# The moving operands of a two-layer decoder trunk 32 bytes past a multiple of 2 KB

## The chip, the cores and the metric

The kernel runs on one core of a Trainium2 chip. The metric is the device time of one execution in microseconds (us). Times come from runs of the kernel on the chip; the profile and the trace come from one more execution, recorded by the hardware profiler. The five engines are TensorE (PE, and PEld for its weight loads), VectorE (DVE), ScalarE (ACT), GpSimd (POOL) and SyncE (SP), which here only issues DMAs.

## The reference

The input x is one sequence of 256 tokens of width 2048, in float32. Two layers follow one another:

```
h = x
layer 0: h += gmlp_chunk_mixer(rms_norm(h))       # 2048 -> 4096 (u, v), gelu, layer norm of v,
                                                  # 16 causal 128x128 token mixes, u * v', 2048 -> 2048
         h += conv_ffn(rms_norm(h))               # gate and up 2048 -> 5632, causal conv of 3 taps
                                                  # on the gate, silu(gate) * up, down 5632 -> 2048
layer 1: h += dilated_attention_mixer(rms_norm(h))# qkv 2048 -> 9216, partial rotary, 3 dilations x
                                                  # 8 heads, merged by softmax, 1024 -> 2048
         h += conv_ffn(rms_norm(h))
out = rms_norm(h)
```

Everything is float32 in and out. The products with the stacked weights are nearly all of the work: each weight is read once, and multiplies 256 tokens.

## The kernel before

**Layout.** Activations are kept transposed: a block is 128 features (partitions) by 256 tokens, so a width of 2048 is KT = 16 blocks and the FFN's 5632 are FB = 44. Weights are tiles of 128 x 128, streamed in units of UT = 8 tiles (512 KB, 784 units in all) through a ring of RING = 4 slots.

**Split products.** Every float32 weight tile and every activation block is split in a high and a low part (float32r). ScalarE writes the high part of a weight unit (`w_hi`, L440), VectorE the rest (`w_lo`, L730). A block of activations has 512 columns: 256 of the high part, then 256 of the low part. For each weight tile TensorE runs a pair (in `multiply`, L1030 and L1031): the high weights times all 512 columns, then the low weights times the first 256. The columns are the moving operand, the weights the stationary one, which a weight load brings in ahead of each product. Both products add up in one PSUM bank.

**The moving operands.** There are four, each of blocks of 512 x 4 = 2048 bytes in each partition (`row` in the code, which is that number of bytes). `X` (16 blocks) is the normalised input of the U, V, gate, up and QKV products; `hid` (44 blocks) is the hidden layer of the FFN; `GX` (16) is the gated product of the mixer and `OX` (8) the output of attention. X has a place of its own. The other three are laid over the same memory, the arena, at different times, by `place`, which adds its offset to `arena_at`; the arena also holds V, U, WS, BS, QK, VT, swap, rope, sm, pt, mask, out_sb and smaller things. `Y`, the last layer's output before its transposes, is laid over X. All of them stand at offsets from `arena_at` that are multiples of 32 bytes, and hid, GX and OX at multiples of 2 KB.

**Addresses.** `lead` pads the start of the allocation to a multiple of 2 KB. Then come raw, w_hi and w_lo (4 slots each of 4 KB), h (16 blocks of 1 KB), X and the arena, so that each of these begins on a multiple of 2 KB. Behind them are vecs (1856 bytes), rinv, std, ssum and the other small buffers.

**Order.** The stages are products one after another: V, U with the token mixes between its units, the mixer's output product, the FFN (`product`, then `down`), eight attention heads, the output product of attention, the second FFN, and final transposes with the stores. Each engine has its own program; they meet in semaphores only. SyncE loads unit n + 4 once VectorE is through with unit n (`lo_ready`); ScalarE splits a unit when TensorE has freed its slot (`units_done`), two units ahead of TensorE. Between splits ScalarE and VectorE take the sums of finished blocks out of PSUM, norm them (X's writers are L460, L564 and L746), and run the conv and silu of the FFN (hid's writers are L519 and L790). GpSimd sums squares. The 30 warm-up products (L1086) run before the first weights are there.

Of the kernel before, what the change touches and what calls it, by code (L numbers as in the profile page):

```python
# [31 lines left out]
F32R = mybir.dt.float32r  # L32
BF16 = mybir.dt.bfloat16
ACT = mybir.ActivationFunctionType
ALU = mybir.AluOpType
AX_X = mybir.AxisListType.X

P = 128
S = 256
D = 2048  # L40
KT = D // P
FFN = 5632
FB = FFN // P
# [41 lines left out]
X_LOADS = (2, 2, 4, 4, 4)  # L85


FIRST = 4 * KT // UT
FIRST_KT = UT // 2

# [22 lines left out]
def one(c):  # L113
    return bass.ds(c, 1)
# [18 lines left out]
def trunk(nc, w_stream, x_t, vecs_d, ws_t, bs_row, mask_d, rope_d, out):  # L133
    with ExitStack() as ctx:
        def sb(name, shape, dt=F32):
            return ctx.enter_context(nc.sbuf_tensor(name, shape, dt))
# [5 lines left out]
        row = 2 * S * 4  # L142
# [3 lines left out]
        w_hi = [sb(f"w_hi{i}", [P, UC], F32R) for i in range(RING)]  # L146
        w_lo = [sb(f"w_lo{i}", [P, UC], F32R) for i in range(RING)]
        h = sb("h", [P, KT, S])
        x_at = nc.sbuf_base
        X = sb("X", [P, KT, 2 * S], F32R)  # L150
        arena_at = nc.sbuf_base
        arena_bytes = FB * 2 * S * 4
        sb("arena", [P, FB * 2 * S])
        assert x_at % row == 0 and arena_at % row == 0

        vecs = sb("vecs", [P, VECS])
        rinv = sb("rinv", [P, S])
# [158 lines left out]
        def vec(c):  # L316
            return vecs[:, c:c + 1]
# [114 lines left out]
        def _(act):  # L432
# [22 lines left out]
            def norm_pair(n, pr):  # L455
# [3 lines left out]
                for b in range(2):  # L459
                    nc.scalar.activation(X[:, 2 * pr + b, 0:S], h[:, 2 * pr + b, :], ACT.Copy,  # L460
                                         scale=vecs[:, one(GAINS[n] + 2 * pr + b)]).then_inc(x_hi, 1)
# [8 lines left out]
            def gelu_evac(pair, pr, stage, s, dst, done):  # L470
                if stage == 0:
                    high_copy(pair, s, done)
                if stage == 1:
                    act.wait_ge(pair_taken, pair + 1)
                    settled()
                    nc.scalar.activation(dst[:, pair_of(pr), :], gu[:, :, 2:S + 2], ACT.Gelu_apprx_tanh)\
                        .then_inc(gelued, 1)
# [83 lines left out]
            for load, n in enumerate(X_LOADS):  # L561
                act.wait_ge(x_landed[load], 16)
                for _ in range(n):
                    nc.scalar.activation(X[:, b, 0:S], h[:, b, :], ACT.Copy, scale=vec(GAINS[0] + b)).then_inc(x_hi, 1)  # L564
                    b += 1
# [9 lines left out]
            for s in range(6, 12):  # L575
                split_step(U_V, s)
                if s == 7:
                    act.wait_ge(ss_added, NORM_PAIRS)
                    gelu_evac(P_V, 0, 0, 0, V, U_V + FIRST - 1)
                if s == 8:  # L580
                    rms(0)
                if s == 9:
                    gelu_evac(P_V, 0, 1, 0, V, U_V + FIRST - 1)
                if s in (10, 11):
                    gelu_evac(P_V + 1, 1, s - 10, 1, V, U_V + FIRST)
            with act.Fori(1, KT // 4) as i:
# [136 lines left out]
        def _(dve):  # L723
# [19 lines left out]
            def x_low(n, pr):  # L743
                for b in range(2):
                    dve.wait_ge(x_hi, KT * n + 2 * pr + b + 1)
                    nc.vector.scalar_tensor_tensor(X[:, 2 * pr + b, S:2 * S], h[:, 2 * pr + b, :],  # L746
                                                   vecs[:, one(GAINS[n] + 2 * pr + b)], X[:, 2 * pr + b, 0:S],
                                                   ALU.mult, ALU.subtract).then_inc(x_ready, 1)
# [271 lines left out]
        def _(pe):  # L1020
            def multiply(u, slot, tiles, needs=None):


                pe.wait_ge(lo_ready, u + 1)
                for n, (bank, moving, kt, first, last) in enumerate(tiles):
                    if needs:
                        needs(kt)
                    hi = w_hi[slot][:, n * P:(n + 1) * P]
                    lo = w_lo[slot][:, n * P:(n + 1) * P]
                    nc.tensor.matmul(bank, hi, moving[:, kt, :], start=first, stop=False)  # L1030
                    op = nc.tensor.matmul(bank[:, S:2 * S], lo, moving[:, kt, 0:S], start=False, stop=last)  # L1031
                op.then_inc(units_done, 1)
# [7 lines left out]
            def two_pairs(u, pair, moving, k_tiles, needs=None, after=None):  # L1040

                per = 2 * k_tiles // UT
                for n in range(2 * per):
                    if n % per == 0:

                        wait_pos(pe, pair_summed, pair + n // per - 1)
                    multiply(u + n, n % RING, tiles_of(n // per, moving, k_tiles, n % per),
                             needs if n < k_tiles // UT else None)
                    if after:
                        after(n)  # L1050

            def mean_square(n):

                pe.wait_ge(ss_added, NORM_PAIRS * (n + 1))
                for b in range(2):
                    op = nc.tensor.matmul(misc[:, 0:S], mean_w[:, :], ssum[:, b * S:(b + 1) * S],
                                          start=(b == 0), stop=(b == 1))
                op.then_inc(ms_ready, 1)

            def normed_ready(n):  # L1060
                return lambda kt: pe.wait_ge(x_ready, KT * n + kt + 1)
# [26 lines left out]
            pe.wait_ge(ident_set, 1)  # L1088
            for u in range(FIRST):
                p, at = u % 2, u // 2 * FIRST_KT  # L1090
                multiply(U_V + u, u % RING, [(acc[p][:, b, :], X, kt, kt == 0, kt == KT - 1)
                                             for kt in range(at, at + FIRST_KT) for b in range(2)], normed_ready(0))
                if u == FIRST - 1:
                    mean_square(0)
            with pe.Fori(1, KT // 4) as i:
                two_pairs(U_V + FIRST * i, P_V + 2 * i, X, KT)

# [262 lines left out]
```

## Time and profile before

| | |
|---|---|
| time before, median of 3 runs | 2290.17 us (2274.45 to 2306.97) |
| profiled execution, its own time | 2290.41 us |
| profiled execution, span | 2288.7 us |
| mean granted TensorE clock | 0.999 of full speed |
| busy: PE, PEld, DVE, ACT, POOL | 99%, 87%, 65%, 56%, 5% |
| mean DMA rate | 183 GB/s |

The span runs from the first to the last instruction of the profiled execution; its own time is the span with the little that lies around it. Busy shares are of the span. TensorE's products are pipelined: the start of one comes before the recorded end of the one ahead, so their durations overlap, and the spacing of starts is what adds up. A few records of products can be missing.

### The profile page before, as it was taken

How to read it: one execution, taken by the hardware profiler on the slowest of the kernel's cores; microseconds unless marked ns; L12 is line 12 of the kernel's file. 1: busy time of each engine (PE TensorE's matmuls, PEld its weight loads, DVE VectorE, ACT ScalarE, POOL GpSimd, SP SyncE). 2: the span in 40 equal slices, each digit the busy share in tenths (PEclk: the TensorE clock that was granted, in tenths of full speed). 3: DMA queues.
4: the chain of work that ended last, by engine and by line, in shares of the span. 5: the costliest groups of instructions: out<-in, count | busy, mean ns of one | idle time of the engine just before them, and what ended most of it. 6: DMA issues, size and time to landing. Idle time of an engine off the chain costs nothing.

```text
span 2288.7 us, 38101 instructions
## 1 busy us (share of the span) xinstructions
PE 2271.0 (99%) x13098; PEld 1988.4 (87%) x13098; DVE 1483.0 (65%) x1764; ACT 1274.1 (56%) x1587; POOL 105.7 (5%) x85
## 2 busy tenths in 40 slices
PE   8999999999999999999999999999999999999998
PEld 7888888888888888888888888888888888888887
DVE  6578666677666655557666666687666666654443
ACT  6455466666666644345555555556666666654443
POOL 3122100000000000000000000020000000000000
PEclk9999999999999999999999999999999999999999
DMA  7544555555555555555554544445555555555553
GB/s 261 199 150 157 193 196 190 191 185 191 190 188 192 187 180 193 194 191 182 176 172 167 172 166 171 160 166 193 183 184 186 188 184 185 188 186 184 187 188 130
DMA packets 115477, 419.21 MB, mean 183 GB/s; under 512 B 12832, under 2 KB 12960, under 8 KB 115168
## 3 DMA queue, kind: packets, MB, share of 16 engines
q1 hardware_dynamic: 114192, 413.43, 52.8%
q0 software_dynamic: 512, 2.95, 0.3%
q10 hardware_dynamic: 720, 2.10, 0.2%
q8 instruction: 37, 0.61, 0.1%
q14 instruction: 16, 0.13, 0.0%
HBM read 416.33 MB, written 2.10 MB: 183 GB/s over the span
## 4 chain that ended last, share of the span: by engine, by line
PE 96%; POOL 1%; DVE 1%; ACT 1%; issue 1%; DMA 0%; DVEq 0%; ACTq 0%; SPq 0%; POOLq 0%
PE acc L1030 61%; PE acc L1031 31%; POOL vsum L403 1%; POOL ssum L378 0%; PE sc_ps L1175 0%; PE sc_ps L1155 0%; PE sc_ps L1162 0%; DMA raw<-w_stream 0%; DVE X L746 0%; PE acc L1218 0%; PE sc_ps L1170 0%; PE sc_ps L1154 0%; PE misc L1146 0%; ACT X L564 0%; ACT w_hi L440 0%
## 5 line engine op out<-in xcount | busy, mean ns | idle before, releaser
L1030 PE MATMUL acc<-X,w_hi 128*128 128x512 f32 x4480 | 1578.9, 397 | 5.1 <-DVE w_lo L730 3.8
L730 DVE TENSOR_TENSOR w_lo<-raw,w_hi 128x1024 fp32r<-128x1024 f32 x784 | 969.2, 1242 | 528.4 <-ACT w_hi L440 527.9
L1031 PE MATMUL acc<-X,w_lo 128*128 128x256 f32 x4480 | 1255.1, 280 | 0.0
L440 ACT ACTIVATE w_hi<-raw 128x1024 fp32r<-128x1024 f32 x784 | 826.2, 1059 | 461.2 <-PE acc L1031 450.3
L1030 PEld LDWEIGHTS acc<-X,w_hi 128*128 128x128 f32 x4480 | 840.9, 188 | 202.6 <-DVE w_lo L730 4.8
L1031 PEld LDWEIGHTS acc<-X,w_lo 128*128 128x128 f32 x4480 | 846.7, 189 | 0.4
L1030 PE MATMUL acc<-hid,w_hi 128*128 128x512 f32 x1408 | 492.9, 395 | 0.0
L1031 PE MATMUL acc<-hid,w_lo 128*128 128x256 f32 x1408 | 394.8, 280 | 0.0
L1030 PEld LDWEIGHTS acc<-hid,w_hi 128*128 128x128 f32 x1408 | 263.9, 187 | 61.9
L1031 PEld LDWEIGHTS acc<-hid,w_lo 128*128 128x128 f32 x1408 | 266.0, 189 | 0.0
L450 ACT ACTIVATE hc<-acc 128x512 f32<-128x512 f32 x104 | 62.3, 599 | 159.6 <-PE acc L1031 159.6
L735 DVE TENSOR_TENSOR tsum<-hc,acc 128x512 f32<-128x512 f32 x104 | 71.5, 687 | 100.2 <-ACT hc L450 100.2
L368 POOL TENSOR_TENSOR ssum<-ssum,sq 128x512 f32<-128x512 f32 x24 | 33.1, 1377 | 1277.3 <-ACT sq L453 1277.3
L1030 PE MATMUL acc<-GX,w_hi 128*128 128x512 f32 x256 | 89.0, 392 | 1.1 <-DVE GX L867 1.1
L510 ACT ACTIVATE conv<-gu,vecs 128x256 f32<-128x256 f32 x88 | 53.4, 606 | 62.8 <-DVE gu L752 62.8
L752 DVE TENSOR_TENSOR gu<-tsum,rinv 128x512 f32<-128x512 f32 x104 | 72.4, 696 | 3.6
L1031 PE MATMUL acc<-GX,w_lo 128*128 128x256 f32 x256 | 71.6, 280 | 0.0
L634 ACT ACTIVATE hc<-acc 128x512 f32<-128x512 f32 (+1 forms) x40 | 22.3, 557 | 81.9 <-PE acc L1031 81.9
L460 ACT ACTIVATE X<-h,vecs x48 | 21.9, 505 | 72.9 <-DVE h L766 72.6
L1030 PEld LDWEIGHTS acc<-GX,w_hi 128*128 128x128 f32 x256 | 47.9, 187 | 11.8 <-DVE GX L867 1.4
L440 ACT ACT_TABLE_LOAD x44 | 56.5, 1283 | 0.9
L515 ACT ACT_TABLE_LOAD x44 | 56.5, 1283 | 0.8
(141 smaller groups left out, 1065.0 us busy)
## 6 DMA issues: line engine op xcount, KB each, us to landing
raw<-w_stream SPq DMA_DIRECT2D x784, 512.0 KB, 3.3
out<-out_sb SPq DMA_DIRECT2D x8, 256.0 KB, 2.8
h<-x_t ACTq DMA_DIRECT2D x3, 512.0 KB, 10.2
WS<-ws_t POOLq DMA_DIRECT2D x1, 1024.0 KB, 5.1
BS<-bs_row POOLq DMA_DIRECT2D x1, 1024.0 KB, 8.2
mask<-mask_d POOLq DMA_DIRECT2D x1, 576.0 KB, 3.9
h<-x_t ACTq DMA_DIRECT2D x2, 256.0 KB, 5.0
rope<-rope_d POOLq DMA_DIRECT2D x1, 256.0 KB, 3.0
```

The source lines that it names most:

```text
L368: nc.gpsimd.tensor_tensor(ssum[:, :], ssum[:, :], sq[:, :, :].rearrange("p a b -> p (a b)"), ALU.add).then_inc(ss_added, 1)
L403: nc.gpsimd.tensor_tensor(vsum[:, :, :], vsum[:, :, :], U[:, 12 + 2 * k:14 + 2 * k, :], ALU.add)\
L440: nc.scalar.activation(w_hi[slot][:, :], raw[slot][:, :], ACT.Copy).then_inc(hi_ready, 1)
L450: nc.scalar.activation(hc[:, :, :], acc[s][:, :, 0:S], ACT.Copy).then_inc(hcopied, 1)
L510: nc.scalar.activation(conv[:, :], gu[:, 0, 2:S + 2], ACT.Identity, bias=vecs[:, one(cv + 3 * FB + j)], scale=vecs[:, one(cv + 2 * FB + j) ...
L515: nc.scalar.activation(act_g[:, :], conv[:, :], ACT.Silu).then_inc(silued, 1)
L634: nc.scalar.activation(hc[:, 0:n, :], acc[(par + m) % 2][:, 0:n, 0:S], ACT.Copy).then_inc(hcopied, 1)
L730: nc.vector.tensor_tensor(w_lo[slot][:, :], raw[slot][:, :], w_hi[slot][:, :], ALU.subtract)\
L735: nc.vector.tensor_tensor(tsum[:, :, :], hc[:, :, :], acc[s][:, :, S:2 * S], ALU.add)\
L752: nc.vector.tensor_tensor(gu[:, :, 2:S + 2], tsum[:, :, :], over(rinv, 2), ALU.mult)\
L1030: nc.tensor.matmul(bank, hi, moving[:, kt, :], start=first, stop=False)
L1031: op = nc.tensor.matmul(bank[:, S:2 * S], lo, moving[:, kt, 0:S], start=False, stop=last)
```

## The change

X's address and the arena's are worked out from one allocation (`moving`), which is 64 bytes longer than the two together. `x_at` is the allocator's base plus SKEW = 32 bytes, and `arena_at` follows X directly. X, and by way of `place` all that lies in the arena, with hid, GX and OX, starts 32 bytes later in each partition than before, as does Y. Weights and h stay where they were. vecs and everything behind it start 64 bytes later.

```diff
@@ -85,6 +85,9 @@
 X_LOADS = (2, 2, 4, 4, 4)
 
 
+SKEW = 32
+
+
 FIRST = 4 * KT // UT
 FIRST_KT = UT // 2
 
@@ -146,12 +149,12 @@
         w_hi = [sb(f"w_hi{i}", [P, UC], F32R) for i in range(RING)]
         w_lo = [sb(f"w_lo{i}", [P, UC], F32R) for i in range(RING)]
         h = sb("h", [P, KT, S])
-        x_at = nc.sbuf_base
-        X = sb("X", [P, KT, 2 * S], F32R)
-        arena_at = nc.sbuf_base
-        arena_bytes = FB * 2 * S * 4
-        sb("arena", [P, FB * 2 * S])
-        assert x_at % row == 0 and arena_at % row == 0
+        x_at = nc.sbuf_base + SKEW
+        arena_at = x_at + KT * row
+        arena_bytes = FB * row
+        sb("moving", [P, (KT + FB) * 2 * S + 16])
+        X = nc.alloc_sbuf_tensor_at("X", [P, KT, 2 * S], F32R, offset=x_at)
+        assert x_at % row == SKEW and arena_at % row == SKEW
 
         vecs = sb("vecs", [P, VECS])
         rinv = sb("rinv", [P, S])
```

## Rows read from the trace of the kernel before

**Rows 1.** The page: span, then busy us (share of the span) and instructions by engine.
```profile
span 2288.7 us, 38101 instructions
PE 2271.0 (99%) x13098; PEld 1988.4 (87%) x13098; DVE 1483.0 (65%) x1764; ACT 1274.1 (56%) x1587; POOL 105.7 (5%) x85
```

**Rows 2.** The page: the chain that ended last, shares of the span by line.
```profile
PE acc L1030 61%; PE acc L1031 31%; POOL vsum L403 1%; POOL ssum L378 0%; PE sc_ps L1175 0%; PE sc_ps L1155 0%; PE sc_ps L1162 0%; DMA raw<-w_stream 0%; DVE X L746 0%; PE acc L1218 0%; PE sc_ps L1170 0%; PE sc_ps L1154 0%; PE misc L1146 0%; ACT X L564 0%; ACT w_hi L440 0%
```

**Rows 3.** Groups of TensorE: form xcount | busy us, mean ns | idle before us, releaser.
```profile
L1030 PE MATMUL acc<-X,w_hi 128*128 128x512 f32 x4480 | 1578.9, 397 | 5.1 <-DVE w_lo L730 3.8
L1030 PE MATMUL acc<-hid,w_hi 128*128 128x512 f32 x1408 | 492.9, 395 | 0.0
```

**Rows 4.** Groups of VectorE's and ScalarE's weight splits, same columns.
```profile
L730 DVE TENSOR_TENSOR w_lo<-raw,w_hi 128x1024 fp32r<-128x1024 f32 x784 | 969.2, 1242 | 528.4 <-ACT w_hi L440 527.9
L440 ACT ACTIVATE w_hi<-raw 128x1024 fp32r<-128x1024 f32 x784 | 826.2, 1059 | 461.2 <-PE acc L1031 450.3
```

**Rows 5.** Timeline of PE at 600 us: start us, duration us, instruction.
```profile
600.00 0.39 PE L1030 MATMUL acc<-X,w_hi 128*128 128x512 f32 x1
600.23 0.28 PE L1031 MATMUL acc<-X,w_lo 128*128 128x256 f32 x1
600.34 0.39 PE L1030 MATMUL acc<-X,w_hi 128*128 128x512 f32 x1
...
602.77 0.39 PE L1030 MATMUL acc<-X,w_hi 128*128 128x512 f32 x1
```

**Rows 6.** Timeline of PE at 1800 us.
```profile
1799.92 0.40 PE L1030 MATMUL acc<-X,w_hi 128*128 128x512 f32 x1
...
1802.04 0.40 PE L1030 MATMUL acc<-X,w_hi 128*128 128x512 f32 x1
```

**Rows 7.** Windows: from:to, length, busy us (instructions) by engine, PEclk, DMA.
```profile
500.00:900.00 400.00, 400.00 (x2309) 352.69 (x2309) 259.64 (x318) 237.83 (x288) 4.01 (x3) 1.00 0.55 189
1600.00:2200.00 600.00, 600.00 (x3398) 520.34 (x3397) 376.93 (x457) 351.99 (x423) 6.49 (x5) 1.00 0.54 186
```

**Rows 8.** Windows of L1030 alone: products (x) and weight loads (x).
```profile
0.00:1100.00 1100.00, 1066.38 (x3057) 572.67 (x3057) 1.00 0.55 190
1100.00:2278.00 1178.00, 1131.04 (x3192) 599.56 (x3191) 1.00 0.52 176
```

**Rows 9.** The warm-up in bf16: its row of the timeline, then its group.
```profile
8.23 1.47 PE L1086 MATMUL acc<-warm_b 128*128 128x512 bf16 x6
...
L1086 PE MATMUL acc<-warm_b 128*128 128x512 bf16 x6 | 1.5, 381 | 0.0
```

**Rows 10.** Instructions that write misc: duration ns min/median/max, first and last start.
```profile
L1056 PE MATMUL misc<-ssum,mean_w x16: 377/379/380, 36.5 to 1542.1; 128*128 128x256 f32 x16
L1106 PE MATMUL misc<-vsum,mean_w x4: 378/379/379, 115.1 to 115.7; 128*128 128x256 f32 x4
```

**Rows 11.** Users of gu (as rows 10), then groups of QK and X.
```profile
L752 DVE TENSOR_TENSOR gu<-tsum,rinv x104: 691/692/1073, 39.9 to 2030.1; 128x512 f32<-128x512 f32 x104
L778 DVE SCALAR_TENSOR_TENSOR conv<-gu,vecs,conv x88: 477/479/483, 317.9 to 2031.8; 128x256 f32<-128x256 f32 x88
L781 DVE SCALAR_TENSOR_TENSOR conv<-gu,vecs,conv x88: 483/484/489, 318.5 to 2032.5; 128x256 f32<-128x256 f32 x88
L928 DVE TENSOR_TENSOR QK<-tsum,rinv 128x512 f32<-128x512 f32 x24 | 16.6, 692 | 0.8
L746 DVE SCALAR_TENSOR_TENSOR X<-h,vecs,X x48 | 31.8, 677 | 19.9 <-ACT X L460 19.6
```

**Rows 12.** DMAs (KB each, median us to landing), an issue and its reader.
```profile
out<-out_sb SPq DMA_DIRECT2D x8, 256.0 KB, 2.8
BS<-bs_row POOLq DMA_DIRECT2D x1, 1024.0 KB, 8.2
L381 POOL DMA_DIRECT2D BS<-bs_row x1: 536/536/536, 33.1 to 33.1; - x1
L861 DVE TENSOR_TENSOR V<-sc_ps,BS x8: 416/418/421, 162.3 to 207.3; 128x256 f32<-128x256 f32 x8
```

## The prediction, on record before the changed kernel was seen

> **What bounds the kernel now.** I read the page's first part before anything else: TensorE is busy 99% of the span, its weight loads 87%, VectorE 65%, ScalarE 56% [rows 1]. The chain of waits ends on it too: lines L1030 and L1031, the two products of each weight tile, are 92% of the span in the chain [rows 2]. The groups of instructions say how that busy time is made: 4480 pairs read X and 1408 read hid, each a 512-column and a 256-column product, and TensorE is idle only 5 us ahead of them [rows 3]; GX and OX take the rest of the 6272 pairs that 784 units of 8 tiles make [rows 4]. The rest hides: VectorE's split into w_lo spends 528 us waiting for ScalarE, and ScalarE's w_hi 461 us, nearly all for TensorE, which has yet to free the slot [rows 4]. So whoever predicts this change predicts the spacing of TensorE's pairs, and nothing else can move the time by a per cent unless it grows by hundreds of us.
>
> I then measured that spacing, because durations of pipelined matmuls overlap and don't add up. Starts of successive L1030 in the timeline are 0.34 to 0.35 us apart at 600 us: 8 pairs from 600.00 to 602.77, that is 346 ns [rows 5]. At 1800 us they are 6 pairs from 1799.92 to 1802.04, 353 ns, at the same full granted clock [rows 6, 7]. Counting agrees: 2309 products in 400 us are 346.5 ns a pair, 3398 in 600 us are 353.1 [rows 7]. The reader is to see two steady spacings 6.6 ns apart, in stages whose operands lie at the same offsets and run the same code (the FFN of layer 0, then that of layer 1). TensorE was in the tighter one before the attention stage and in the looser one behind it. With 3057 pairs before 1100 us and 3192 behind [rows 8] (these records lack 23 of the 6272), a run that kept the tight spacing would take 3192 x 6.6 ns = 21 us less, 2269 us; one that was loose throughout 3057 x 6.6 = 20 us more, 2311 us. The three times shown, 2274 to 2307, fill just this interval. Which spacing a stage falls into is thus worth up to 42 us from run to run with no change to the kernel.
>
> **The sum's base.** The profiled execution took 2290.4 us by its own time, 1.7 us above its span [rows 1], and the median of the runs is 2290.2. They agree, so I work on 2290.
>
> **The change, part by part.** No instruction, wait, queue or DMA is added or removed. Only addresses move: X, hid, GX, OX, and all else in the arena, by 32 bytes; vecs, rinv, ssum and what follows them by 64.
>
> *TensorE's moving reads.* All 12544 reads of the main products start 32 bytes later. The stride between blocks stays 2048 bytes, so every L1030 read, which covered one aligned 2 KB piece, now crosses from one to the next; the L1031 reads (1 KB) stay inside one. No full-rate float32r read at an odd offset is in the trace, so I bound it. From below: the six warm-up products in bf16 with the same 512 columns have spacing (1.47 - 0.38)/5 = 218 ns [rows 9], against 230 for L1030 (600.00 to 600.23) and 117 for L1031 (600.23 to 600.34) [rows 5]. So 12 ns of each float32r 512-column product come with its wider element, and about half of that of the 256-column one. If the shift freed all of it, 18 ns a pair, 6272 x 18 = 113 us would go. From above: nothing in the rows limits a loss; the nearest step is the one between the two spacings, 6.6 ns a pair. If each of the two reads of a pair paid one such step, 13.2 ns x 6272 = 83 us would come. Half-rate float32 reads do not react to a position like this: the mean squares read ssum, which lies 1856 bytes past a multiple of 2 KB by the layout, and the means read vsum on a multiple of 1 KB; both have 379 ns [rows 10]. But they have slack that the full-rate reads lack. What I take: the 12 ns belong to something per piece of the row read, and a shifted read touches one piece more. With pieces of 64 bytes that is 12/32 = 0.4 ns, with 128 bytes 12/16 = 0.75 ns; twice a pair, 6272 times, 5 to 9 us. I take +5, nearer to zero than to either bound, since the spacing was so far the same wherever X and hid are read, in 64 different blocks.
>
> The Trainium skill, page "SBUF — State Buffer", section "Specifications (TRN2)", gives SBUF lines of 16 bytes; 32 bytes are two of them, so a shifted read touches as many lines as before, and by that rule this term is 0 and the sum 2290. No run here shows the size of a line.
>
> *Writes and reads of ScalarE and VectorE.* 64 + 88 + 16 blocks are written in two halves each, and read back. The trace has unaligned neighbours: gu is written 8 bytes past its row by L752 in 692 ns, and QK, on a multiple of 1 KB, by L928 in 692; conv from gu at 4 bytes (L778) takes 479 ns, at 0 (L781) 484 [rows 11]. I cost these at nothing. What hides them anyway is the 528 and 461 us of waiting [rows 4]; without that cover a 1% longer split would cost 10 us of VectorE time, but raw, w_hi and w_lo don't move. The uncovered places are the ends of products, where X's last blocks are awaited: VectorE's wait for X is 20 us over 48 instructions [rows 11], and 1% of its own 32 us is nothing.
>
> *DMAs.* BS, the slowest into the arena, lands 8.2 us after its issue at 33 us, and its first reader comes at 162 us [rows 12]. Doubling it still hides, and WS, mask and rope are issued tens of us ahead of their readers too. Only the out stores stand on the path: 8 of 256 KB from the arena, 2.8 us from issue to landing, and the last one ends the span [rows 12]. Between 0 and 3 us (a landing doubled), or a few tenths less than nothing if such a read happened to be quicker; I take 0. The Trainium skill, page "DMA: Bandwidth & Descriptors", section "How a descriptor splits into AXI transactions", has a descriptor that starts off a 256-byte boundary pay for a partial first transaction; for rows of 2048 bytes that is 9 transactions in place of 8, an estimate of 0.35 us on a 2.8 us landing. It speaks against the change, and the trace can't show it, since every store in it is aligned.
>
> *The small names behind the arena* stay on multiples of 64 bytes relative to one another; [rows 10] shows ssum off 128 already. Zero.
>
> Sum: 2290 + 5 + 0 + 0 = **2295 us**.
>
> **Forecast, and its range.** No change in kind (chance 0.63): two spacings of about 347 and 354 ns, mixed by chance. From all tight, 2269, to all loose with one more piece a read, 2311 + 9 = 2320: its own range is 2265 to 2320. A difference under 2%, some 46 us, is what I count as no change; with 42 us of spread in the kernel itself, a measurement of it tells little less.
>
> **Rival 1, slower: each moving read pays a whole step more** (0.25). Place: the start, or the crossing at the end, of every read of L1030 and L1031. For it: TensorE does lose time to how its full-rate reads fall, the 6.6 ns between [rows 5] and [rows 6], and weight loads and moving reads, which now start on like boundaries, would be out of step. Against it: 4 and 8 bytes cost the other engines nothing. Price: 6.6 ns for each of two reads, 13.2 ns a pair; 2269 + 83 = 2352 from the tight spacing, 2290 + 83 = 2373 from today's mix. It decides from 46 us / 6272 = 7.3 ns a pair on: if only one of the reads pays, the time stays at 2310 to 2331 and counts as no change.
>
> **Rival 2, faster: the two read streams disturb each other now** (0.12). TensorE reads weights and moving columns at once (PEld 87% busy, [rows 1]), both from multiples of 512 bytes; 32 bytes apart they might interleave. For it: the 12 ns over bf16 are unexplained, and two spacings in one code look like two ways for two streams to lock. Against it: the loss goes with the columns (13 or so of 230 ns, half of it in the 117), while there is one weight load for each product whatever its columns. Price: the whole 18 ns gives 2290 - 113 = 2177; a third of it, with the loose spacing gone too, 2269 - 38 = 2231. It decides at 7.3 ns a pair. The Trainium skill, page "TensorE: Matmul & The Clock Gate", section "Wait — 56ns, not 53.3ns?", puts the spacing at columns over 2.4 GHz plus 2.5 ns, which is 216 and 109 ns; the bf16 rows come near (218), the float32r rows don't.
>
> **Rival 3, inside the forecast: the shift only changes which spacing a stage locks to.** All tight 2269, all loose 2311; I give it no chance of its own, as its times are no change. That the edit doesn't do what it says is out: hid, GX and OX are all placed from arena_at, at multiples of 1 KB, and X at x_at.
>
> **How the numbers follow.** 2295 is the likeliest case's. For 8 in 10, the range must reach into both rivals: down to 2250, past which lies most of rival 2, and up to 2360, which holds the lower half of rival 1. Outside are some 0.10 on each side. Faster 0.12, same 0.63, slower 0.25.
>
> **What would show it.** Spacing of pairs in the FFN stages: 346 to 354 ns for the forecast; 360 or more for rival 1, in L1030 alone if the crossing counts and in L1031 too if the start does; below 340 for rival 2, with L1030 under 230. The number of products in a steady 200 us tells it at once: 1155 or 1133 now [rows 7]. VectorE's and ScalarE's durations on X and hid should stay within 1%, the out landings near 2.8 us. A spacing beyond 360 would mean that a shifted read pays on every piece, not once, which I have no row for.

## The result: no steady stretch has the looser spacing

| | median us | range us | runs |
|---|---|---|---|
| before | 2290.3 | 2274.45 to 2306.97 | 16 |
| changed | 2272.1 | 2270.28 to 2273.59 | 16 |
| ratio changed / before | 0.9919 | [0.9894, 0.9944] | |

The changed kernel is 0.8% faster, 18 us on the medians, which is under 2% and well outside the interval. I had forecast 2295, so the sign of the small move was wrong. The time lies inside my range all the same. Its spread says more than its median: the runs of before cover 32 us, those of the changed kernel 3. Its slowest run is faster than the fastest of before.

The profiled execution took 2273.5 us by its own time, against 2290.4. The page, for [rows 1] (span, then busy us and instructions by engine), and the groups for [rows 3] and [rows 4] (form xcount | busy us, mean ns | idle before us, releaser):

```profile
span 2271.7 us, 38101 instructions
PE 2254.0 (99%) x13098; PEld 2000.2 (88%) x13098; DVE 1482.1 (65%) x1764; ACT 1269.9 (56%) x1587; POOL 105.9 (5%) x85
...
L1033 PE MATMUL acc<-X,w_hi 128*128 128x512 f32 x4480 | 1566.1, 392 | 4.8 <-DVE w_lo L733 2.7
L733 DVE TENSOR_TENSOR w_lo<-raw,w_hi 128x1024 fp32r<-128x1024 f32 x784 | 968.3, 1242 | 517.2 <-ACT w_hi L443 516.9
L443 ACT ACTIVATE w_hi<-raw 128x1024 fp32r<-128x1024 f32 x784 | 824.9, 1058 | 448.8 <-PE acc L1034 437.6
L1033 PE MATMUL acc<-hid,w_hi 128*128 128x512 f32 x1408 | 488.2, 390 | 0.0
```

(L1033 and L1034 are the lines that were L1030 and L1031.) VectorE's busy time is what it was and ScalarE's is 4 us less; TensorE's fell by 17 us, which is the whole gain between the two profiled executions. The windows of the changed kernel, for [rows 7], show where:

```profile
500.00:900.00 400.00, 400.00 (x2309) 354.61 (x2308) 259.57 (x318) 237.49 (x288) 4.03 (x3) 1.00 0.59 189
1600.00:2200.00 600.00, 600.00 (x3464) 531.91 (x3463) 380.13 (x458) 351.94 (x424) 6.49 (x5) 1.00 0.59 189
```

The reader is to compare the counts in brackets: 2309 products between 500 and 900 us, as before; 3464 between 1600 and 2200 us, against 3398. The FFN of layer 1 has the spacing of layer 0's now, 600/3464 x 2 = 346.4 ns. The windows of L1033 alone, for [rows 8], add up to the gain: the last 3191 pairs take 1161 us in place of 1178, the first 3058 take 1100 as they did. The FFN of layer 1 is 2112 of these pairs, 14.1 us at 6.7 ns each; most of the rest is in the QKV products, which the heads' small products interrupt.

```profile
0.00:1100.00 1100.00, 1066.27 (x3058) 574.77 (x3059) 1.00 0.58 190
1100.00:2261.00 1161.00, 1112.98 (x3191) 599.45 (x3190) 1.00 0.56 179
```

Something did move inside the pair, even at 600 us, where the spacing is the same. The timeline of the changed kernel (start us, duration us), for [rows 5]:

```profile
599.90 0.39 PE L1033 MATMUL acc<-X,w_hi 128*128 128x512 f32 x1
600.13 0.28 PE L1034 MATMUL acc<-X,w_lo 128*128 128x256 f32 x1
...
602.68 0.39 PE L1033 MATMUL acc<-X,w_hi 128*128 128x512 f32 x1
```

8 pairs in 2.78 us. From the starts in the trace, in ns: the steady pair was 230 + 117 and is 228 + 118, both 346.7 in sum. The loose pair of before ran, near 1800 us, through 233 + 117, 241 + 120, 236 + 113, three different pairs that repeat, 353.3 on average. The changed kernel's trace has no steady stretch like that.

### The profile page after: what moved, and what is told of

Same layout as the page of the kernel before. It is cut to its first block, busy times and chain, and to the rows that moved or that the text cites. A ratio compares the mean times of both kernels' runs of the same rounds, so it can differ in the third digit from the quotient of the medians.

```text
span 2271.7 us, 38101 instructions
## 1 busy us (share of the span) xinstructions
PE 2254.0 (99%) x13098; PEld 2000.2 (88%) x13098; DVE 1482.1 (65%) x1764; ACT 1269.9 (56%) x1587; POOL 105.9 (5%) x85
## 4 chain that ended last, share of the span: by engine, by line
PE 96%; POOL 1%; ACT 1%; DVE 1%; issue 0%; DMA 0%; DVEq 0%; SPq 0%; ACTq 0%; POOLq 0%
PE acc L1033 61%; PE acc L1034 32%; POOL vsum L406 1%; POOL ssum L381 0%; PE sc_ps L1178 0%; PE sc_ps L1158 0%; PE sc_ps L1165 0%; DMA raw<-w_stream 0%; PE acc L1221 0%; PE sc_ps L1173 0%; PE sc_ps L1157 0%; PE misc L1149 0%; ACT X L567 0%; ACT w_hi L443 0%; ACT U L605 0%
## 5 line engine op out<-in xcount | busy, mean ns | idle before, releaser
L1033 PE MATMUL acc<-X,w_hi 128*128 128x512 f32 x4480 | 1566.1, 392 | 4.8 <-DVE w_lo L733 2.7
L733 DVE TENSOR_TENSOR w_lo<-raw,w_hi 128x1024 fp32r<-128x1024 f32 x784 | 968.3, 1242 | 517.2 <-ACT w_hi L443 516.9
L1034 PE MATMUL acc<-X,w_lo 128*128 128x256 f32 x4480 | 1264.2, 282 | 0.0
L1033 PEld LDWEIGHTS acc<-X,w_hi 128*128 128x128 f32 x4480 | 842.4, 188 | 181.2 <-DVE w_lo L733 3.4
L1034 PEld LDWEIGHTS acc<-X,w_lo 128*128 128x128 f32 x4480 | 848.2, 189 | 0.5
L1033 PE MATMUL acc<-hid,w_hi 128*128 128x512 f32 x1408 | 488.2, 390 | 0.0
L1034 PE MATMUL acc<-hid,w_lo 128*128 128x256 f32 x1408 | 397.1, 282 | 0.0
L1033 PEld LDWEIGHTS acc<-hid,w_hi 128*128 128x128 f32 x1408 | 264.3, 188 | 55.4
L1034 PEld LDWEIGHTS acc<-hid,w_lo 128*128 128x128 f32 x1408 | 266.1, 189 | 0.0
L1033 PE MATMUL acc<-GX,w_hi 128*128 128x512 f32 x256 | 89.0, 391 | 1.1 <-DVE GX L870 1.1
L1034 PE MATMUL acc<-GX,w_lo 128*128 128x256 f32 x256 | 72.2, 282 | 0.0
L1033 PEld LDWEIGHTS acc<-GX,w_hi 128*128 128x128 f32 x256 | 48.0, 188 | 11.5 <-DVE GX L870 1.4
```

The costliest lines, as they stand in the source:

```text
L733: nc.vector.tensor_tensor(w_lo[slot][:, :], raw[slot][:, :], w_hi[slot][:, :], ALU.subtract)\
```

## Experiments

Two theories stood at first. **A:** what counts is where the moving reads lie against the weight reads. **B:** what counts is where a moving read starts, whatever the weights do.

**1. Everything 32 bytes on; weights alone 32 bytes on.** One kernel undoes the relative shift, the other turns it round.

```diff
 # e1_all32, against the changed kernel; e2_weights32 has the first line too
-        sb("lead", [P, (-(-(-nc.sbuf_base // 64) * 64) % row) // 4])
+        sb("lead", [P, (-(-(-nc.sbuf_base // 64) * 64) % row) // 4 + SKEW // 4])
...
-        x_at = nc.sbuf_base + SKEW
+        x_at = nc.sbuf_base
 # e2_weights32: vecs and a pad ahead of h bring x_at back to a multiple of 2 KB
```

> Weights, h, X, arena and all behind them 32 bytes past a multiple of 2 KB, so that nothing has moved against the weights. Theory A (what counts is where moving reads lie against weight reads): as the kernel before, both spacings, 347 and 353 ns a pair, and runs spread over 2274 to 2307 us. Theory B (what counts is that a moving read starts off 64 bytes, whatever the weights do): as the changed kernel, 347 ns throughout, all runs within 2270 to 2274 us.

> raw, w_hi and w_lo 32 bytes past a multiple of 2 KB, X and the arena on it. Theory A (relative position): as the changed kernel, 347 ns throughout and 2270 to 2274 us, if 32 bytes the other way round serve as well. Theory B (the moving read's own start): as the kernel before, both spacings, 2274 to 2307 us.

Measured: e1 2301.5 us (2289.5 to 2302.9), ratio 1.0075 [1.0044, 1.0107] to before; e2 2308.8 us (2308.7 to 2310.3), ratio 1.0115 [1.0076, 1.0155]. Moved together with the weights, X's 32 bytes bring no gain, and B falls. With the weights 32 bytes on and X where it was, there is harm: e2's six runs all stand within 3 us of the 2311 that the prediction had for every stage loose. A window of its TensorE alone, 567 pairs in 200 us or 353 ns, and the same window of e1:

```profile
500.00:700.00 200.00, 200.00 (x1134) 1.00 0.55 187
500.00:700.00 200.00, 200.00 (x1134) 1.00 0.54 184
```

A holds, but not in the form "32 bytes apart": the direction counts. Nor is it the whole. By A, e1 should have drawn as the kernel before; 8 of its 9 runs took 2300 to 2303 us (its trace has both FFNs loose), while none of the 14 runs of before beside them was over 2294.6. So where level operands stand, or something else that e1 moved (raw, h, the small buffers), weighs on the draw between the two spacings. Which of these it is was not tested.

**2. Pairs of products with nothing beside them.** Six kernels run such pairs from fixed operands and compute nothing of the reference: 64 pairs (or single products) in a stretch, 12 stretches of each case, with a few products of varying width between stretches, so that each starts at another phase. In these stretches ScalarE and VectorE have no instruction and no data is loaded or stored. Each case of a kernel writes its own PSUM bank. Like cases agree across banks: those with the moving reads 32 bytes ahead are the first, second or last case of their kernel, and (0; 0; 0) is a first case too.

```python
for i in range(PAIRS):                       # shortened; m, w_: offsets in elements
    k = i % 8
    matmul(bank, w_hi[:, 128 * k + w_:][:, :128], X[:, 512 * k + m:][:, :512], ...)
    matmul(bank[:, S:2 * S], w_lo[:, 128 * k + w_:][:, :128], X[:, 512 * k + m:][:, :S], ...)
```

> Only pairs of products from fixed operands, nothing else on the core: 7 cases of offsets (moving, weights) in bytes: (0,0), (32,0), (64,0), (128,0), (0,32), (32,32), (1024,0), 64 pairs each, 12 times over, each time begun at another phase. It computes nothing of the reference. Theory A: (0,0), (32,32), and (64,0), (128,0), (1024,0) if lines are 64 bytes, are found at 353 ns a pair in part of their stretches; (32,0) and (0,32) never. Theory B: (0,0), (0,32), (64,0), (128,0), (1024,0) are, (32,0) and (32,32) never. Rival C (the looser spacing needs ScalarE, VectorE or DMA beside TensorE): all cases at 347 ns only.

> As m1, other offsets (moving; w_hi; w_lo) in bytes: (64; 32; 32), (32; 64; 64), (96; 0; 0), (48; 0; 0), (32; 0; 32), (32; 32; 0), (0; 480; 480). It computes nothing of the reference. Theory A, relative offset alone counts: (64; 32; 32) as (32, 0) in m1, 347 ns in all 12; (32; 64; 64) as (0, 32), both spacings; (0; 480; 480), which is 32 ahead modulo 512, 347 ns in all 12 if the place within 512 bytes counts. The mixed ones tell whether w_hi's or w_lo's place matters: the one that keeps 347 ns in all 12 names the read that counts.

Measured: ns a pair, from the last 23 spacings of a stretch, and in how many of the 12.

| moving; w_hi; w_lo (bytes) | ns a pair (stretches) |
|---|---|
| 0; 0; 0 (before) | 353.3 (10), 346.7 (2) |
| **32; 0; 0 (changed)** | **346.7 (12)** |
| 64; 32; 32 | 346.7 (12) |
| 0; 480; 480 | 346.7 (12) |
| 32; 32; 32 (e1) | 346.7 (7), 353.3 (5) |
| 0; 32; 32 (e2) | 346.7 (7), 353.3 (5) |
| 32; 64; 64 | 353.3 (11), 346.7 (1) |
| 1024; 0; 0 | 353.3 (11), 346.7 (1) |
| 64; 0; 0 | 353.3 (10), 348.8 (2) |
| 48; 0; 0 | 350.2 to 351.1 (7), 346.5 (5) |
| 96; 0; 0 | 350.0 (12) |
| 128; 0; 0 | 351.0 (12) |
| 32; 0; 32 | 344.5 (5), 346.7 (4), 353.3 (3) |
| 32; 32; 0 | 353.1 (12) |

In the trace of m1, the third timeline row of a stretch of case (0; 0; 0), called aa, and its last, then the same of (32; 0; 0), ab:

```profile
183.97 0.39 PE L102 MATMUL aa<-X,w_hi 128*128 128x512 f32 x1
...
204.82 0.40 PE L102 MATMUL aa<-X,w_hi 128*128 128x512 f32 x1
...
207.02 0.40 PE L102 MATMUL ab<-X,w_hi 128*128 128x512 f32 x1
...
225.75 0.39 PE L102 MATMUL ab<-X,w_hi 128*128 128x512 f32 x1
```

From aa's row to the last that the window holds are 59 pairs in 20.85 us, 353 ns; from ab's, 54 in 18.73, 347 ns. Three things follow. The loose spacing needs no other engine, so rival C of the expectation falls. At one place of the moving reads against the weights, 32 bytes ahead, it does not occur in any of the 12 stretches, and the same holds where both lie 32 bytes further on (64; 32; 32). Theory A had wrongly expected that of (0; 32; 32) too. And 480 bytes behind is as good as 32 ahead, so it is the place within some span of at most 512 bytes that counts. Both weight reads take part: with w_hi 32 behind and w_lo level, even 344.5 ns appears; the other way round, 353.1 always.

**3. Single products, short weight loads, and smaller offsets.**

> As m1, other cases: 512-column products alone at moving offset 0 and 32, with weight loads of 32 columns instead of 128, 256-column products alone at 0 and 32, pairs at 16 and at 4 bytes. It computes nothing of the reference. If weight reads slow moving reads, the 512-column product with the short weight load starts every 216 to 220 ns against about 230 with the full load; if the extra 12 ns belong to float32r reads themselves, both have 230. Pairs at 16 and 4 bytes: as at 32 (347 ns only) if any start off 64 bytes serves; otherwise both spacings.

> Pairs with weight loads of 32 columns at (0; 0) and (32; 0), and single products of 384, 448, 504 and 192 columns, and of 512 at 96 bytes. It computes nothing of the reference. m2 had 226.7 ns for 512 columns and 116.7 to 120 for 256, which are 34 and 17.5 to 18 slots of 6.67 ns, against 32 and 16 for the columns alone. Theory F (each product costs two slots whatever its columns): 384 columns 173.3 ns, 448 200.0, 504 223 to 227. Rival G (a loss for each column, as my prediction had it): 6% over the columns, 170, 198.5 and 223 ns, off the grid of 6.67. If weight reads cause the looser spacing, the pair with short loads at (0; 0) never shows it; if it shows it all the same, they don't.

Measured, settled ns from start to start: 512 columns alone 226.7 at offset 0, 233.3 at 32 and at 96, 226.7 for 504 columns, 231.7 for 512 with weight loads of 32 columns; 448 columns 202.5 (10) or 206.7 (2); 384 columns 173.3; 256 columns 120.0 at offset 0, 116.5 to 117.7 at 32; 192 columns 111.7. In m2's timeline (64 products a row):

```profile
130.98 14.75 PE L102 MATMUL ba<-X,w_hi 128*128 128x512 f32 x64
145.96 15.14 PE L102 MATMUL bb<-X,w_hi 128*128 128x512 f32 x64
161.34 14.97 PE L102 MATMUL bc<-X,w_hi 128*32 128x512 f32 x64
176.55 7.88 PE L105 MATMUL bd<-X,w_lo 128*128 128x256 f32 x64
184.67 7.68 PE L105 MATMUL be<-X,w_lo 128*128 128x256 f32 x64
```

bb is the shifted case of ba, 15.14 against 14.75 us: alone, a 512-column product is slower when shifted; be against bd shows the 256-column one to be faster. The lone spacings don't predict the pair: shifted they add up to 350 ns or a little more (233.3 and about 117), and the shifted pair takes 346.7. Over their columns at 2.4 GHz (213.3, 160 and 106.7 ns) the unshifted products of 512, 384 and 256 columns all cost 13.3 ns more, which speaks for theory F, one sum for each product, and against one for each column. But F isn't the whole: 504 columns cost 16.7 ns more, 192 columns 31.7, and 448 columns fit neither F (200.0) nor G (198.5). A short weight load, which should only help if weight reads were mere traffic, slowed the lone 512-column product (231.7 against 226.7, where I expected 216 to 220). Pairs with short loads at (0; 0) took 343.3 (4) or about 348.3 ns (8) and never 353. At (32; 0) they took 346.1 to 347.3 (11) and once 353.3, so with short loads 32 bytes ahead is not proof against the loose spacing. The length of the load thus changes the spacing, but these products also write only 32 partitions, so the load alone isn't shown to be the cause. Pairs at 16 bytes: 346.7 (10), 360.0 (2); at 4 bytes: 359.8 (8), 353.3 (4). At such small offsets, then, it can get worse than the 353.3 of the kernel before.

**4. Another skew in the full kernel; X alone; the arena alone.**

```diff
-SKEW = 32                                    # e3_skew64
+SKEW = 64
```
```diff
-        arena_at = x_at + KT * row           # e4_x_only
...                                           # vecs and a pad, up to 2 KB, ahead of the arena
+        arena_at = nc.sbuf_base
```
```diff
-        x_at = nc.sbuf_base + SKEW           # e7_arena_only
-        arena_at = x_at + KT * row
+        x_at = nc.sbuf_base
+        arena_at = x_at + KT * row + SKEW
```

> The changed kernel with SKEW 64 in place of 32. Theory A (moving reads 32 bytes ahead of weight reads are the one good place; m1 showed 353 ns in 10 of 12 stretches at 64): most of the FFN at 353 ns, 2300 to 2311 us. Rival D (any shift off the multiple of 2 KB serves, since a read then crosses one): 347 ns throughout, 2270 to 2274 us.

> X 32 bytes past a multiple of 2 KB, the arena with hid, GX and OX on it. Theory A: 347 ns (228 and 118) wherever X is read, while the two down products, which read hid, may take either spacing: times 2271 to 2281 us, since 1408 pairs at 6.7 ns are 9.4 us. Rival E (what the stretch before left behind decides, not the operand's place): X's stages of layer 1 loose in some runs, times up to 2307 us.

> The arena (hid, GX, OX) 32 bytes past a multiple of 2 KB, X on it: the other half of the change. Theory A: the products that read X (4480 of 6272 pairs, the FFN's 1408 of each layer among them) take either spacing, each layer's gate and up products by themselves, hid's are at 346.7 always; times 2271 to 2275 us with none loose, about 2280 to 2286 with one layer (1408 pairs x 6.7 ns = 9.4 us), up to 2301 with all of X's. Rival E (a stage keeps the spacing that the stage before left it): as the kernel before, groups near 2276, 2292 and 2307 us, 15 us apart, hid's products loose with X's.

Measured: e3 2289.0 us (2284.1 to 2290.4), ratio 1.0004 [0.9966, 1.0043]: no gain, so rival D falls. So does theory A's 2300 to 2311: its FFNs stood at 348.9 ns, the rarer of the two spacings of m1 at 64. e4 2271.8 us (2271.6 to 2273.5), ratio 0.9953 [0.9925, 0.9982]: the same as the changed kernel. e7 2298.8 us (2288.4 to 2300.5), ratio 1.0040 [0.9998, 1.0081]: nothing gained. **X's 32 bytes carry the gain.** The windows of TensorE in e7's trace are two of gate and up products (500, 1700 us) and two of down products (820, 2100 us):

```profile
500.00:700.00 200.00, 200.00 (x1133) 1.00 0.57 186
820.00:1000.00 180.00, 180.00 (x1040) 1.00 0.57 190
1700.00:1900.00 200.00, 200.00 (x1134) 1.00 0.56 185
2100.00:2200.00 100.00, 100.00 (x579) 1.00 0.59 188
```

353, 346, 353 and 345 ns a pair: where X stands level with the weights the spacing is loose, and where hid is shifted it is tight, in one run. In e4's windows the down products, whose hid stands level there, are tight too:

```profile
820.00:1000.00 180.00, 180.00 (x1041) 1.00 0.56 190
```

and no run of e4 was over 2273.5 us, where loose down products of one layer would have added 704 x 6.7 = 4.7 us. Its product that reads GX, level as well, is loose, 353.5 ns a pair, between X's tight stages:

```profile
215.00:285.00 70.00, 70.00 (x396) 1.00 0.55 184
```

So at level offsets both spacings can last. The down products follow the gate and up products without a pause, and at level offsets they had their spacing each time (before, e1, e4), which is rival E for these alone; in e7 hid stands 32 ahead and they turn tight at once. With whole weight loads and both weight reads 32 behind, only the tight one lasted in any run. This fits the runs of the kernel before. In the 87 shown beside the changed kernel and the experiments they stand in three groups, near 2276 us (40), 2291 us (29) and 2306 us (18): 15 us is one layer's FFN, gate, up and down, 2112 pairs x 6.7 = 14.1 us. Read so, none, one or both layers fell into the loose spacing (only one of these runs has a trace: 2290.4 us, layer 1 alone loose). The other 87 x 2 - 29 - 36 = 109 of the 174 FFNs stayed tight, although bare pairs at the same offsets were loose in 10 stretches of 12.

**5. Is there a better place?** m5 and m6 went on from (32; 0; 32).

> As m3, (moving; w_hi; w_lo): (32; 0; 64), (64; 32; 0), (64; 0; 64), (96; 64; 0), (96; 0; 96), (32; 64; 0), (32; 0; 96). It computes nothing of the reference. If w_hi's place alone made 353 ns go, all cases with w_hi 32 behind the moving reads (the first, second, fourth and last) have 347 ns or less; if each weight read must be 32 behind, they have 350 or more in part.

> As m5: (32; 0; 128), (128; 96; 0), (16; 0; 16), (48; 0; 48), (32; 0; 16), (256; 0; 0), (288; 0; 0). It computes nothing of the reference. (0; 480; 480) behaved as (32; 0; 0) in m3. If the place within 512 bytes counts, (288; 0; 0) shows 353 ns in some stretches; if within 256 or less, (288; 0; 0) is as (32; 0; 0), 347 ns in all 12, and (256; 0; 0) as (0; 0; 0), mostly 353.

| moving; w_hi; w_lo | ns a pair (stretches) |
|---|---|
| **64; 0; 64** | **340.0 (5), 350.0 (7)** |
| 32; 0; 96 / 32; 0; 128 / 288; 0; 0 | 346.7 to 347 (12 each) |
| 32; 0; 16 / 32; 64; 0 | 346.7 or 347 (10 each), 353.3 (2) / 350.0 (2) |
| 48; 0; 48 / 96; 64; 0 | 346.7 (7 / 6), 350.0 (5) / 353.3 (6) |
| 32; 0; 64 / 128; 96; 0 / 96; 0; 96 / 16; 0; 16 | 349.0 / 348.6 / 349.3 / 350.7 (11 or 12 each) |
| 64; 32; 0 / 256; 0; 0 | 353.3 (12) / 353.3 (8), 346.7 (4) |

(288; 0; 0) is as good as (32; 0; 0), so the span within which the place counts is 256 bytes or less for the moving read; and since 128 and 0, and 96 and 32, are unlike, it isn't 128 or 64. Both rules of m5's expectation fall: w_hi 32 behind does not suffice, since (64; 32; 0) is loose in all 12, and w_lo need not be 32 behind, since (32; 0; 96) never is loose. Two of these went into the full kernel:

```diff
-SKEW = 32                                    # e6_lo64; e5_lo32 keeps 32; moving is resized
+SKEW = 64
...
+        sb("pad", [P, SKEW // 4])            # between w_hi and w_lo, so w_lo and h move too
         w_lo = [sb(f"w_lo{i}", [P, UC], F32R) for i in range(RING)]
         h = sb("h", [P, KT, S])
-        x_at = nc.sbuf_base + SKEW
+        x_at = nc.sbuf_base
```

> The changed kernel with w_lo (and h) moved by 32 bytes too, so that only w_hi's reads lie 32 bytes behind the moving ones, as (32; 0; 32) in m3, which took 344.5 ns in 5 of 12 stretches, 346.7 in 4 and 353.3 in 3. If the full kernel draws from the same set: 2257 us with 344.5 throughout, 2270 with 346.7, 2310 with 353.3, and stage by stage a mix, 2260 to 2295 us and a spread over 5 us. Rival: with all stages at 346.7 or below it beats the changed kernel.

> Moving operands and w_lo (and h) 64 bytes past a multiple of 2 KB, w_hi on it, as (64; 0; 64) in m5, which took 340.0 ns in 5 of 12 stretches and 350.0 in 7. If the full kernel draws from the same two: 2230 us with 340.0 in all stages, 2292 with 350.0, and about 22 us (2112 + some pairs x 10 ns) between runs whose one FFN goes either way; median 2255 to 2290. It beats the changed kernel if its median is under 2270.

Measured: e5 2290.7 us (2278.7 to 2305.4), ratio 0.9985 [0.9943, 1.0026], a lottery as expected, though two of its 12 runs lie above the 2295 that I had as its end. Its profiled execution has 353.3 ns in the FFN of layer 0, 346.7 in that of layer 1 and 344.5 only in GX's and part of OX's product. No gain. **e6 2236.9 us (2233.5 to 2238.3 in 6 runs), ratio 0.9774 [0.9717, 0.9831] to before**, and 35 us under the median of the changed kernel, which ran in another series; no run of either comes within 30 us of the other. It beats both. Its timeline and a window:

```profile
599.85 0.39 PE L1034 MATMUL acc<-X,w_hi 128*128 128x512 f32 x1
600.08 0.28 PE L1035 MATMUL acc<-X,w_lo 128*128 128x256 f32 x1
...
602.57 0.39 PE L1034 MATMUL acc<-X,w_hi 128*128 128x512 f32 x1
```
```profile
500.00:700.00 200.00, 200.00 (x1178) 1.00 0.58 194
```

8 pairs in 2.72 us, 340.0 ns, with no switch: the windows of layer 1 count 1178 as well. I had feared the 350 ns that bare pairs took in 7 stretches of 12; of e6's steady stages only the product that reads GX shows it (401 products from 215 to 285 us, 349 ns), and the times of its runs, 5 us apart, leave no room for it in an FFN, where it would cost 2112 x 10 ns = 21 us.

## Why the prediction was wrong

**The bound, right.** The time went with TensorE's spacing. VectorE's w_lo took 1242 ns as before, its writes to hid 418 ns against 419, gu 691 against 692; BS landed in 8.3 us against 8.2, out in 2.9 against 2.8. All terms that I set to zero were zero to 0.1 us. The two spacings and the interval between them were right as well: "a run that kept the tight spacing would take ... 2269 us" against 2272.1 measured.

**The step that failed** is the term of the moving reads: "the 12 ns belong to something per piece of the row read, and a shifted read touches one piece more", +5 us. Measured: 0 ns in a pair that is tight, 346.7 at both offsets, and 6.7 ns less in each steady pair that had been loose, which is the gain. One 512-column product by itself does pay 6.7 ns for the shift (226.7 to 233.3), but the pair does not. I took the excess for one that goes with the columns, because 230 and 117 ns split that way. The split of a pair doesn't tell what each product costs: alone they take 226.7 and 120.0, the same sum split otherwise, and single products of 256, 384 and 512 columns all cost 13.3 ns more than their columns. The same false reading was my argument against rival 2 ("the loss goes with the columns"). Of its mechanism, two read streams that disturb each other, the experiments bear out that the place of one against the other sets the spacing, at a price of 6.7 ns where a stage was loose in place of 18 everywhere; that they lock to each other is my picture of it and isn't shown. One figure of the argument for +5 was miscounted as well: X and hid are 16 + 44 = 60 blocks, not 64, which changes nothing.

**The base under it failed with it.** I kept 2290, a mix of two spacings "mixed by chance", as if the change left the draw alone, and gave the case "the shift only changes which spacing a stage locks to" no chance of its own, since its times lay within 2%. It is what happened. The draw was the only thing in the trace that two stages with the same code and the same offsets did differently, so it was the first thing that a change of offsets could settle, in either direction: e2, the mirror image of the change, settles it the other way, at 2308.8 us. That 2272.1 fell inside the range is owed to the 2269 of the all-tight case, not to the sum.

**One stream's lines, or two streams.** The Trainium skill, page "SBUF — State Buffer", section "Specifications (TRN2)", gives lines of 16 bytes, so 32 bytes are two whole lines and by that rule would change nothing. Such a shift gave 2272.1 us one way (the changed kernel) and 2308.8 the other (e2), so a count of one stream's lines is not enough here. The Trainium skill, page "TensorE: Matmul & The Clock Gate", section "Step-by-step: what each phase is for", says that loading the next weights takes no read bandwidth from the running matmul. Here the place of the weights alone changes the spacing of float32r pairs: (32; 0; 0) was tight in 12 stretches of 12, (32; 32; 32) in 7. The two reads are thus not independent of each other's place; whether they share bandwidth, no run shows.

**What stays open.** What the two reads share; why 32 bytes ahead has a single lasting pattern; what decides the draw at level offsets, and why e1 and e7 drew loose stages so much more often than the kernel before; and why FFNs draw the loose spacing less often than bare pairs (65 of 174 against 10 of 12). The same bare case in several places of PSUM, bf16 pairs, and offsets of w_hi and w_lo beyond those in the tables weren't tried.

## What to carry to other kernels

When a kernel is bound by back-to-back products, measure their spacing from starts, stage by stage, and look for two values of it under the same code: a run-to-run spread in discrete steps is a sign of the same. Then move the moving operand and the weights against each other by 32 and 64 bytes; it costs a pad, and here it was worth 0.8% and 2.3% against a kernel that drew its spacing by chance. Against that kernel's own best runs, near 2274.5 us, the 32 bytes are worth only 0.1%. Scan the offsets with bare pairs, but let the full kernel decide, as it drew 340 ns where they drew 350 more often, and 353 where they drew 344.5.

## What was not expected of the hardware

- Many mean spacings of steady float32r products at the full granted clock are multiples of 3.33 ns (8 cycles at 2.4 GHz): 120.0, 173.3, 226.7 and 233.3 ns for one product, 340.0, 346.7, 350.0 and 353.3 for a pair. Others are not: 111.7, 202.5 and 231.7 for one, 344.5, 348.9 and 351.0 for a pair. In the loose stretch of before even 353.3 is a mean over three unlike pairs.
- A product's spacing depends on its neighbours: 226.7 + 120.0 alone, 230 + 117, 228 + 118 or 227 + 113 (e6) in a pair.
- At level offsets a steady pattern outlives the stage: the down products kept what the gate and up products had, in each layer of the traces of before, e1 and e4.
